# Split operands, one gate buffer and a later load of x in the stage that mixes the two branches of a diffusion layer

## The chip, the cores and the metric

The kernel runs on one core of one Trainium2 chip. The metric is the device time of one launch in microseconds (us). The profile is one execution of the same kernel, taken by the hardware profiler; its span is the time from the first to the last instruction.

## The reference, cut to what matters

One layer works on 1280 tokens (256 context tokens, 1024 latent ones) of 1024 features, all in float32. Two branches, an RWKV scan (`y_a`, 512 features) and an attention (`y_b`, 512 features), are projected, gated, summed and projected again. Then comes a feed-forward part of 2816 features.

```python
y_a, s_fin = rwkv_branch(r, k, v, xw, xa, xg, s0, lp)      # ends with a group norm, a bonus term and a gate
mixed = jax.nn.sigmoid(ga) * (y_a @ lp['w_out_a']) + jax.nn.sigmoid(gb) * (merge_heads(y_b) @ lp['w_out_b'])
x = x + g1 * (mixed @ lp['w_out'])
h2 = rmsnorm(x, lp['norm2_g']) * (1 + sc2) + sh2
x = x + g2 * conv_ffn(h2, lp)
```

The change is inside the line `mixed = ...`: two products with weights of 512 x 1024 each, for 1280 tokens.

## The kernel before, in words

Features lie on the 128 partitions and tokens along the free axis. So `y_a` (`ya`) and `y_b` (`yb4`) are 4 tiles of 128 x 1280 each, and `mixed` (`mix`) has 8 such tiles. A product for one output tile goes over the tokens in three segments (`SEGS`: 256, 512 and 512 columns), each with a PSUM bank of its own.

Two ways of multiplying are used. Most weight tiles (the input projection, `w_out`, the feed-forward part) go through `split_mm` (lines 876 to 880). Both operands are kept as a high part in the type float32r and a low part, the rest, in the same type. Three matmuls are issued for each product: high x high, high x low, low x high. The high parts of a weight are made by a multiplication with ones on GpSimd (line 2366) and the rest by a subtraction there (line 2367). Both are in `split_tile(s, loads, used, src)`. It waits for the load of the tile into one of the two buffers `raw[0]`, `raw[1]`, then for `w_used` (the PE has finished with the pair `hi[s]`, `lo[s]`), and counts up `w_split`. The mix alone multiplies plain float32: `mix_block(n)` (line 1347) takes its weights straight from `raw[q]` and its data from `ya` and `yb4`, 4 tiles deep for 3 segments, first the a half (q = 0), then the b half (q = 1). So 2 x 8 halves of 12 products each make the whole stage. The profile shows each float32 matmul as two records.

What stands around it, in the order of the PE's queue:

- Group norm of the scan's output (lines 1300 to 1341). For each of the 4 tiles j of `ya` the PE spreads the inverse deviations (`gn`, line 1338) and computes the gate (`gate`, line 1326). VectorE scales (line 2207, reads one SBUF tile and PSUM), adds bias and bonus (line 2210, reads two SBUF tiles) and multiplies by the gate (line 2213, SBUF and PSUM). `ya_ready` counts the last of these, `gn_out` the first. ScalarE has its last work of this stage at line 1771. GpSimd has none.
- The mix (lines 1347 to 1361). VectorE multiplies each half by its sigmoid gate from PSUM (line 2227, 3 instructions a half), adds the two (line 2233, two SBUF tiles) and counts `mix_ready`. ScalarE rounds the tile to its high part `mixH` (line 1779) and VectorE subtracts (line 2219, `mix_rest`, two SBUF tiles), one block later.
- The projection `w_out` (lines 1375 to 1398): 8 blocks of `split_mm`. In block n = 0 the loop over the 8 tiles k of `mix` is outermost, each waiting for its `mix_split`. From n = 1 on, the PE also transposes the input `x` (`x_again`) to features first, between the segments (line 1371).

SyncE issues all loads of this stretch in one fixed order. `load_mix(n, q)` brings one half's weights (256 KB) into the first half of `raw[q]`. `load_gates(n)` brings two tiles of 640 KB (line 817), into one of two buffers of two tiles each; it waits for `mix_ready` of the block two back. Five of the ten row blocks of `x` (512 KB each) are loaded behind block 1 of the mix (line 827), where their memory is free, and the other five behind the second load of `w_out` (line 840). That second load waits for the last matmul of the mix.

The memory of this stretch is packed. `gates` takes 4 tiles of 1280 words from `FREE + KB*T`, `x_again` lies over the same 8 tiles' space, `mixH` takes the 8 tiles ahead of it and `mix` the 8 behind it.

## Time and profile before

| what | value |
|---|---|
| time, median of 3 runs | 2513.81 us (2509.5, 2513.81, 2513.95) |
| profiled execution | 2510.51 us, span 2508.7 us |
| PE busy | 2377.6 us, 95% of the span |
| VectorE, ScalarE, GpSimd busy | 1302.6, 727.7 and 657.9 us |
| granted TensorE clock, mean | 0.983 of 2.4 GHz |
| traffic with memory | 234.5 MB, 93 GB/s over the span |

Engines are PE (TensorE matmul), PEld (its weight loads), DVE (VectorE), ACT (ScalarE), POOL (GpSimd) and SP (SyncE, which issues the loads; SPq is its queue). "L1354" is line 1354. In a timeline a row has start and duration in us, engine, line, operation, output<-inputs with shapes, the number of instructions merged into the row and, in brackets, how long the engine was idle before it and what released it. Matmuls are pipelined. One instruction's duration is longer than the distance to the next one's start, and the distance is what the engine spends.

### The profile page before, as it was taken

To read this page: it belongs to the slowest core of one execution; us is meant where nothing else is said; L and a number is where in the kernel's file an instruction comes from. 1 tells how busy PE (TensorE), PEld (TensorE's weight loads), DVE (VectorE), ACT (ScalarE), POOL (GpSimd) and SP (SyncE) were. 2 spreads that over 40 slices of the span, in tenths; PEclk is the share of its full clock that TensorE was granted. 3 is DMA by queue.
4 is the path that set the end of the run, shared out by engine and by line. 5 is a ranking of instruction groups with operands and counts; after the bars stand their busy time and mean duration, and the time that the engine had idled before them with its cause. 6 is when DMAs were issued, how large, how long until landed. Compare 5 with 4: busy or idle time off the path is not lost.

```text
span 2508.7 us, 50664 instructions
## 1 busy us (share of the span) xinstructions
PE 2377.6 (95%) x21610; PEld 1953.1 (78%) x21610; DVE 1302.6 (52%) x2069; ACT 727.7 (29%) x1193; POOL 657.9 (26%) x283
## 2 busy tenths in 40 slices
PE   5899999999999998889999998999999999999997
PEld 4677878788888887888855587788888888888885
DVE  4565657537468667895543424733333433343344
ACT  5273644544455553333300001301100110011002
POOL 1121020111111111222100144344344434444341
PEclk9899999999999999999989999999999999999999
DMA  6213121021366776676503311011111111111112
GB/s 281 89 46 115 45 70 62 28 94 66 103 193 188 207 203 206 178 215 178 178 31 133 130 43 34 26 43 34 43 34 42 40 37 43 34 43 34 43 34 93
DMA packets 224561, 234.53 MB, mean 93 GB/s; under 512 B 143922, under 2 KB 178866, under 8 KB 222898
## 3 DMA queue, kind: packets, MB, share of 16 engines
q1 hardware_dynamic: 199090, 229.55, 28.4%
q10 hardware_dynamic: 25344, 3.15, 0.8%
q8 instruction: 97, 1.59, 0.3%
q14 instruction: 30, 0.25, 0.0%
HBM read 173.80 MB, written 57.02 MB: 92 GB/s over the span
## 4 chain that ended last, share of the span: by engine, by line
PE 81%; DVE 9%; issue 3%; ACT 2%; DMA 2%; SPq 1%; ACTq 1%; POOL 1%; DVEq 0%; POOLq 0%
PE PS L878 19%; PE PS L880 19%; PE PS L879 19%; PE PS L1354 5%; PE PS L1022 3%; PE PS L994 2%; DVE buffer L2080 2%; DVE buffer L2081 2%; PE PS L1008 1%; PE PS L996 1%; PE PS L1326 1%; PE PS L1164 1%; PE PS L1074 1%; DMA buffer<-in_w_ada_first 1%; ACTq L1723 1%
## 5 line engine op out<-in xcount | busy, mean ns | idle before, releaser
L878 PE MATMUL PS<-buffer,buffer 128*128 128x512 f32 (+1 forms) x2784 | 994.6, 357 | 17.0 <-DVE buffer L2265 6.0
L880 PE MATMUL PS<-buffer,buffer 128*128 128x512 f32 (+1 forms) x2784 | 990.1, 356 | 0.0
L879 PE MATMUL PS<-buffer,buffer 128*128 128x512 f32 (+1 forms) x2784 | 987.3, 355 | 0.0
L878 PEld LDWEIGHTS PS<-buffer,buffer 128*128 128x128 f32 x2784 | 526.4, 189 | 106.1 <-issue 23.2
L879 PEld LDWEIGHTS PS<-buffer,buffer 128*128 128x128 f32 x2784 | 526.7, 189 | 78.0 <-issue 1.0
L880 PEld LDWEIGHTS PS<-buffer,buffer 128*128 128x128 f32 x2784 | 526.5, 189 | 73.2
L2366 POOL TENSOR_TENSOR buffer<-buffer,buffer 128x1024 fp32r<-128x1024 f32 x76 | 183.9, 2420 | 816.2 <-PE PS L880 506.3
L2309 DVE SCALAR_TENSOR_TENSOR buffer<-PS,buffer,buffer 128x512 f32<-128x512 f32 (+1 forms) x264 | 158.5, 656 | 148.3 <-PE PS L880 148.3
L2367 POOL TENSOR_TENSOR buffer<-buffer,buffer 128x1024 fp32r<-128x1024 f32 x76 | 194.2, 2556 | 6.0
L2285 DVE TENSOR_SCALAR buffer<-buffer,buffer 128x1281 f32<-128x1281 f32 x22 | 34.8, 1581 | 282.3 <-ACT buffer L1810 282.3
L1810 ACT ACTIVATE buffer<-PS 128x512 f32<-128x512 f32 (+1 forms) x66 | 30.1, 529 | 498.1 <-PE PS L880 498.1
L2379 POOL TENSOR_TENSOR buffer<-buffer,buffer 128x1024 fp32r<-128x1024 f32 x28 | 71.8, 2564 | 352.7 <-ACT buffer L1620 352.7
L1354 PE MATMUL PS<-buffer,buffer 128*128 128x512 f32 (+1 forms) x384 | 137.8, 521 | 0.8 <-DVE buffer L2213 0.8
L1354 PEld LDWEIGHTS PS<-buffer,buffer 128*128 128x128 f32 x384 | 72.9, 190 | 66.4 <-issue 60.7
L1022 PE MATMUL PS<-buffer,buffer 128*128 128x128 f32 x832 | 107.7, 277 | 4.3 <-DVE buffer L1976 4.3
L2348 POOL TENSOR_TENSOR buffer<-buffer,buffer 128x1024 fp32r<-128x1024 f32 x12 | 29.6, 2469 | 305.2 <-DMA buffer<-in_w_in 255.4
L1022 PEld LDWEIGHTS PS<-buffer,buffer 128*128 128x128 f32 x832 | 99.6, 192 | 6.9 <-DVE buffer L1976 6.9
L2388 POOL TENSOR_TENSOR buffer<-buffer,buffer 128x512 f32<-128x512 f32 x40 | 53.0, 1347 | 192.9 <-PE PS L1220 177.5
L1859 DVE CUSTOM_DVE_ANT_0 PS<-buffer,buffer 128x1024 f32<-128x1024 f32 x64 | 78.9, 1233 | 25.6 <-DMA buffer<-in_w_ada 21.1
L2294 DVE TENSOR_TENSOR buffer<-buffer,PS 128x512 f32<-128x512 f32 (+1 forms) x66 | 35.6, 594 | 106.8 <-PE PS L880 105.5
L2286 DVE SCALAR_TENSOR_TENSOR buffer<-buffer,buffer,buffer 128x1281 f32<-128x1281 f32 x22 | 77.0, 3502 | 2.6 <-DVE buffer L2285 1.4
L1573 ACT ACTIVATE buffer<-buffer,buffer 128x768 f32<-128x768 f32 (+1 forms) x80 | 67.9, 849 | 32.5 <-DVE buffer L1963 32.4
(226 smaller groups left out, 2793.6 us busy)
## 6 DMA issues: line engine op xcount, KB each, us to landing
buffer<-in_w_up SPq DMA_DIRECT2D x44, 512.0 KB, 3.4
buffer<-in_w_in SPq DMA_DIRECT2D x42, 512.0 KB, 5.3
ops_kept<-buffer SPq DMA_DIRECT2D x40, 512.0 KB, 4.6
buffer<-ops_kept SPq DMA_DIRECT2D x80, 256.0 KB, 3.5
buffer<-in_w_ada SPq DMA_DIRECT2D x32, 512.0 KB, 6.7
buffer<-rkv_kept SPq DMA_DIRECT2D x120, 128.0 KB, 3.4
buffer<-in_w_down SPq DMA_DIRECT2D x22, 512.0 KB, 3.3
buffer<-in_x SPq DMA_DIRECT2D x20, 512.0 KB, 6.9
```

Of the source, the lines that this page charges most:

```text
L878: mm(out, w_hi, x_hi, start=start, stop=False)
L879: mm(out, w_hi, x_lo, start=False, stop=False)
L880: return mm(out, w_lo, x_hi, start=False, stop=stop)
L1022: ins = mm(PS[:, 6, 0:P], src[:, at, :], pT[u % 2][:, b, :], start=(b == 0), stop=(b == nb - 1))
L1354: ins = mm(PS[:, 3 * q + g, 0:m], raw[q][:, k, :], src[:, k, t0:t0 + m], start=(k == 0), stop=(k == NP - 1))
L1573: act.activation(scr[:, u % 3, lo:768], scr[:, u % 3, lo:768], ACT.Exp, bias=rowstat[:, u % 3, 0:1], accum_out=rowstat[:, u % 3, 1:2]).the ...
L1859: return dve.tensor_tensor_reduce(spare, src, silu[:, c, :], 1.0, 0.0, ALU.mult, ALU.add, dst[:, c:c + 1])
L2286: V.link(stt(u, upad[:, odd, 0:ZP - 2], conv_taps("conv_ffn", f, 0), u, ALU.mult, ALU.add))
L2309: ins = stt(x1[:, n, t0:t0 + m], PS[:, 3 * (n % 2) + g, 0:m], mod[:, 40 + n, c:c + 1], x1[:, n, t0:t0 + m], ALU.mult, ALU.add)
L2366: G.link(pool.tensor_tensor(hi[s], src, ones_tile, ALU.mult))
L2367: pool.tensor_tensor(lo[s], src, hi[s], ALU.subtract).then_inc(w_split, 1)
L2379: pool.tensor_tensor(lo[t % 2], raw[t % 2], hi[t % 2], ALU.subtract).then_inc(w_split, 1)
```

## The change

The mix is computed as the other tiles are. Its weights of both halves are loaded into one `raw` buffer and split into `hi`, `lo` on GpSimd. `ya` and `yb4` are split too: the high part by ScalarE (`Copy` into float32r), the rest by GpSimd. `mix_block` uses `split_mm` and computes the b half first. There is one gate buffer of two tiles instead of two buffers. All ten row blocks of `x` are loaded behind the mix. The tile numbers behind the mix grow by 8 (`MIX_TILE`, `WO_TILE`).

```diff
+        ybH = view(FREE + KB * T, NP, T, dtype=F32R)
+        yaH = [view(FREE + (KB + NP) * T, 2, T, dtype=F32R), view(FREE + (KB - 2) * T, 2, T, dtype=F32R)]
+        ybL = view(KK_AT, NP, T, dtype=F32R)
+        yaL = view(LO_AT + NP * T, NP, T, dtype=F32R)
+        gates = view(FREE + (KB + NP + 2) * T, 2, T)
...
 SyncE
+            def load_mix(n):
+                r = (n + 1) % 2
+                if n >= 2:
+                    sp.wait_ge(w_split, MIX_TILE + n - 1)
+                for q in range(2):
+                    sp.dma_start(raw[r][:, q * NP:(q + 1) * NP, :].rearrange("p k n -> p (k n)"),
+                                 dram[("w_oa", "w_ob")[q]][n]).then_inc(w_in[r], 16)
...
             def load_gates(n):
-                if n >= 2:
-                    sp.wait_ge(mix_ready, n - 1)
+                if n == 0:
+                    sp.wait_ge(var_done, 1)
+                else:
+                    sp.wait_ge(mix_ready, n)
                 for q in range(2):
-                    sp.dma_start(gates[:, 2 * (n % 2) + q, :], dram["gates_kept"][q * KB + n]).then_inc(gates_in[n % 2], 16)
+                    sp.dma_start(gates[:, q, :], dram["gates_kept"][q * KB + n]).then_inc(gates_in, 16)
...
+            load_mix(1)
             load_gates(0)
-            load_gates(1)
             for n in range(1, KB):
+                if n + 1 < KB:
+                    load_mix(n + 1)
+                load_gates(n)
+            for n in range(KB):
+                load_tile(n % 2, dram["w_o"][n], WO_TILE + max(n - 1, 0))
                 if n == 1:
+                    for b in range(TB):
+                        if b == 0:
+                            sp.wait_ge(w_used, WO_TILE)
+                        if b == 7:
+                            sp.wait_ge(mix_ready, KB)
                         sp.dma_start(x_again[:, b, :], dram["x"][b]).then_inc(tiles_moved[b // 2], 16)
...
 TensorE
             def mix_block(n):
+                s = n % 2
+                pe.wait_ge(w_split, MIX_TILE + n + 1)
+                for at, (q, part) in enumerate(((1, yb_part), (0, ya_part))):
+                    if n == 0:
+                        pe.wait_ge((gn_out, ya_ready)[at], 3 * NP)
+                        pe.wait_ge(y_split, NP * (at + 1))
+                    else:
+                        pe.wait_ge(mix_out, 2 * n - 1 + at)
                     for g, (t0, m) in enumerate(SEGS):
                         for k in range(NP):
-                            ins = mm(PS[:, 3 * q + g, 0:m], raw[q][:, k, :], src[:, k, t0:t0 + m], start=(k == 0), stop=(k == NP - 1))
+                            x_hi, x_lo = part(k)
+                            ins = split_mm(PS[:, 3 * at + g, 0:m], hi[s][:, q * NP + k, :], lo[s][:, q * NP + k, :],
+                                           x_hi[:, t0:t0 + m], x_lo[:, t0:t0 + m], k == 0, k == NP - 1)
+                    ins.then_inc((mix_mm, w_used)[at], 1)
-            pe.wait_ge(ya_ready, 3 * NP)
-            pe.wait_ge(gn_out, 3 * NP)
-            pe.wait_ge(yb_kept, 32)
...
 ScalarE
+            act.wait_ge(yb_kept, 32)
+            for k in range(NP):
+                act.activation(ybH[:, k, :], yb4[:, k, :], ACT.Copy).then_inc(y_rounded, 1)
+            for k in range(NP):
+                act.wait_ge(ya_ready, 3 * k + 3)
+                act.activation(yaH[k // 2][:, k % 2, :], ya[:, k, :], ACT.Copy).then_inc(y_rounded, 1)
             for k in range(KB):
                 act.wait_ge(mix_ready, k + 1)
+                if k == KB - 2:
+                    act.wait_ge(w_used, WO_TILE)
                 act.activation(mixH[:, k, :], mix[:, k, :], ACT.Copy).then_inc(mix_rounded, 1)
...
 VectorE, mix_products(n): waits for gates_in, 32 * (n + 1); takes the b half first, gates[:, q], PS[:, 3 * at + g]
...
 GpSimd
+            def split_mix(n):
+                split_tile(n % 2, W4 + 2 * (n // 2) + 2, MIX_TILE + n - 1, raw[(n + 1) % 2])
+            def split_y(at, rest, whole, rounded):
+                pool.wait_ge(y_rounded, at)
+                pool.tensor_tensor(rest, whole, rounded, ALU.subtract).then_inc(y_split, 1)
+            split_mix(0)
+            for k in range(NP):
+                split_y(k + 1, ybL[:, k, :], yb4[:, k, :], ybH[:, k, :])
+            for k in range(NP):
+                split_y(NP + k + 1, yaL[:, k, :], ya[:, k, :], yaH[k // 2][:, k % 2, :])
             pool.wait_ge(gate_done, 3 * NP)
+            for n in range(1, KB):
+                split_mix(n)
```

## Rows read from the trace of the kernel before

**Rows 1.** Busy time by stretch: stretch, its length, busy us (count) by engine, granted clock, DMA share, GB/s.
```profile
1261.60:1293.70 32.10, 31.37 (x59) 13.27 (x58) 21.25 (x29) 1.77 (x4) 0.00 (x0) 0.63 0.00 0
1293.70:1431.50 137.80, 137.75 (x386) 73.19 (x387) 43.10 (x58) 8.89 (x7) 4.70 (x2) 1.00 0.31 107
1431.50:1552.70 121.20, 119.63 (x658) 102.72 (x657) 35.35 (x53) 10.62 (x9) 61.12 (x25) 1.00 0.19 66
```

**Rows 2.** The chain that ended last, in order of time (start, us, what), at the mix.
```profile
1293.75 137.76 PE PS L1354 x384
```

**Rows 3.** Groups of instructions by line: busy us, mean ns, idle before.
```profile
L1354 PE MATMUL PS<-buffer,buffer 128*128 128x512 f32 (+1 forms) x384 | 137.8, 521 | 0.8 <-DVE buffer L2213 0.8
```

**Rows 4.** Timeline of the mix.
```profile
1302.64 0.33 SPq L781 DMA_DIRECT2D buffer<-in_w_oa  x1
...
1311.23 0.33 SPq L781 DMA_DIRECT2D buffer<-in_w_ob  x1
...
1328.42 1.62 DVE L2227 TENSOR_TENSOR buffer<-buffer,PS 128x256 f32<-128x256 f32 x3 [6.91 <-PE PS L1354]
1330.08 1.49 DVE L2233 TENSOR_TENSOR buffer<-buffer,buffer 128x1280 f32<-128x1280 f32 x1
...
1331.60 0.80 SPq L817 DMA_DIRECT2D buffer<-gates_kept  x2
```

**Rows 5.** Timeline from the end of the mix.
```profile
1431.18 0.19 PEld L878 LDWEIGHTS PS<-buffer,buffer 128*128 128x128 f32 x1 [0.51 <-POOL buffer L2367]
...
1433.09 0.28 PE L878 MATMUL PS<-buffer,buffer 128*128 128x256 f32 x1
...
1434.61 5.09 DVE L2219 TENSOR_TENSOR buffer<-buffer,buffer 128x1280 fp32r<-128x1280 f32 x2
...
1434.81 0.28 PE L878 MATMUL PS<-buffer,buffer 128*128 128x256 f32 x1
...
1435.90 2.45 POOL L2366 TENSOR_TENSOR buffer<-buffer,buffer 128x1024 fp32r<-128x1024 f32 x1 [4.76 <-DMA buffer<-in_w_o]
...
1438.43 3.54 POOL L2367 TENSOR_TENSOR buffer<-buffer,buffer 128x1024 fp32r<-128x1024 f32 x1
...
1445.18 0.38 PE L1371 MATMUL PS<-buffer,buffer 128*128 128x128 f32 x2
```

**Rows 6.** Timeline of the group norm's end.
```profile
1265.89 1.50 ACT L1771 ACTIVATE buffer<-PS 8x256 f32<-8x256 f32 x3 [3.84 <-PE PS L1153]
...
1269.93 1.55 DVE L2210 SCALAR_TENSOR_TENSOR buffer<-buffer,buffer,buffer 128x1280 f32<-128x1280 f32 x1
...
1273.30 4.64 PE L1326 MATMUL PS<-buffer,buffer 128*128 128x256 f32 x6
...
1277.87 4.63 PE L1338 MATMUL PS<-buffer,buffer 8*128 8x256 f32 x6
...
1286.52 2.41 PE L1338 MATMUL PS<-buffer,buffer 8*128 8x256 f32 x6
...
1288.86 4.11 PE L1326 MATMUL PS<-buffer,buffer 128*128 128x256 f32 x6
...
1293.01 0.69 DVE L2213 TENSOR_TENSOR buffer<-buffer,PS 128x512 f32<-128x512 f32 x1 [0.65 <-PE PS L1326]
...
1293.75 41.52 PE L1354 MATMUL PS<-buffer,buffer 128*128 128x256 f32 x116 [0.78 <-DVE buffer L2213]
```

**Rows 7.** One line's instructions each: duration in ns min/median/max, first and last start.
```profile
L2219 DVE TENSOR_TENSOR buffer<-buffer,buffer x8: 1483/1485/3671, 1331.5 to 1436.0; 128x1280 fp32r<-128x1280 f32 x8
L2442 POOL TENSOR_TENSOR buffer<-buffer,buffer x22: 2890/2962/2981, 1613.2 to 2455.0; 128x1280 fp32r<-128x1280 f32 x22
```

**Rows 8.** Busy time by stretch, columns as in the first group, while gates are loaded.
```profile
1331.60:1337.00 5.40, 5.40 (x14) 2.46 (x13) 1.37 (x1) 1.27 (x1) 0.00 (x0) 1.00 0.66 243
```

**Rows 9.** The loads of the gates: time from issue to landing.
```profile
DMA to landing us min/median/max: 3.2/5.5/13.9
```

**Rows 10.** Busy time by stretch, while `x` is loaded behind the mix.
```profile
1437.00:1441.00 4.00, 4.00 (x22) 3.42 (x21) 2.70 (x1) 0.00 (x0) 3.92 (x2) 1.00 1.03 417
```

More of the change, by code:

```diff
@@ L489, in build @@
         assert FREE + 3 * KB * T == LO_AT
-        gates = view(FREE + KB * T, 4, T)
+        ybH = view(FREE + KB * T, NP, T, dtype=F32R)
[3 more added lines that the diff above has]
+        gates = view(FREE + (KB + NP + 2) * T, 2, T)
         mixH = view(FREE, KB, T, dtype=F32R)
@@ L518, in build @@
         tstat = view(FREE + 6 * D, 2, TB)
-        WO_TILE = len(TILES)
+        MIX_TILE = len(TILES)
+        WO_TILE = MIX_TILE + KB
         FFN_TILE = WO_TILE + KB
@@ L546, in build @@
             sem(n) for n in ("mix_mm", "mix_out", "mix_ready", "mix_rounded", "mix_split"))
-        gates_in = [sem(f"gates_in{s}") for s in range(2)]
+        gates_in = sem("gates_in")
+        y_rounded, y_split = sem("y_rounded"), sem("y_split")
         xt_done, xt_out, x1_out = (sem(n) for n in ("xt_done", "xt_out", "x1_out"))
@@ L795, in _ @@
                     sp.wait_ge(w_split, len(TILES))
-                    load_mix(0, 1)
+                    load_mix(0)
                 if i == 5:
@@ L809, in _ @@
             sp.wait_ge(fin_stored, 16)
-            load_mix(0, 0)
             def load_gates(n):
-                if n >= 2:
-                    sp.wait_ge(mix_ready, n - 1)
+                if n == 0:
+                    sp.wait_ge(var_done, 1)
+                else:
+                    sp.wait_ge(mix_ready, n)
                 for q in range(2):
-                    sp.dma_start(gates[:, 2 * (n % 2) + q, :], dram["gates_kept"][q * KB + n]).then_inc(gates_in[n % 2], 16)
+                    sp.dma_start(gates[:, q, :], dram["gates_kept"][q * KB + n]).then_inc(gates_in, 16)
             sp.dma_start(yb4.rearrange("p j t -> p (j t)"), dram["yb_kept"]).then_inc(yb_kept, 16)
+            load_mix(1)
             load_gates(0)
-            load_gates(1)
             for n in range(1, KB):
-                for q in range(2):
-                    load_mix(n, q)
-                if n == 1:
-                    for b in range(TB // 2, TB):
-                        sp.dma_start(x_again[:, b, :], dram["x"][b]).then_inc(tiles_moved[b // 2], 16)
-                if n + 1 < KB:
-                    load_gates(n + 1)
-            for n in range(KB):
-                if n < 2:
-                    sp.wait_ge(mix_mm, 2 * KB - 1 + n)
-                    load_tile(n, dram["w_o"][n])
-                else:
-                    load_tile(n % 2, dram["w_o"][n], WO_TILE + n - 1)
-                if n == 1:
-                    for b in range(TB // 2):
-                        sp.wait_ge(mix_ready, KB - 1 if b < 2 else KB)
+                if n + 1 < KB:
[3 more added lines that the diff above has]
+                load_tile(n % 2, dram["w_o"][n], WO_TILE + max(n - 1, 0))
+                if n == 1:
+                    for b in range(TB):
[3 more added lines that the diff above has]
+                            sp.wait_ge(mix_ready, KB)
                         sp.dma_start(x_again[:, b, :], dram["x"][b]).then_inc(tiles_moved[b // 2], 16)
@@ L2222, in mix_products @@
                 out = mix[:, n, :]
-                dve.wait_ge(gates_in[n % 2], 32 * (n // 2 + 1))
-                for q, dst in enumerate((out, gates[:, 2 * (n % 2) + 1, :])):
-                    dve.wait_ge(mix_mm, n * 2 + q + 1)
+                dve.wait_ge(gates_in, 32 * (n + 1))
+                for at, (q, dst) in enumerate(((1, gates[:, 1, :]), (0, out))):
+                    if at == 0:
+                        dve.wait_ge(mix_mm, n + 1)
+                    else:
+                        dve.wait_ge(w_used, MIX_TILE + n + 1)
                     for g, (t0, m) in enumerate(SEGS):
-                        ins = tt(dst[:, t0:t0 + m], gates[:, 2 * (n % 2) + q, t0:t0 + m], PS[:, 3 * q + g, 0:m], ALU.mult)
+                        ins = tt(dst[:, t0:t0 + m], gates[:, q, t0:t0 + m], PS[:, 3 * at + g, 0:m], ALU.mult)
                         if g < 2:
@@ L2232, in mix_products @@
                 dve.wait_ge(mix_out, n * 2 + 2)
-                tt(out, out, gates[:, 2 * (n % 2) + 1, :], ALU.add).then_inc(mix_ready, 1)
+                tt(out, out, gates[:, 1, :], ALU.add).then_inc(mix_ready, 1)
             dve.wait_ge(ya_ready, 3 * NP)
```

14 lines of the change are left out of this document (4 added, 10 removed).

## The prediction, made before the changed kernel ran

> **What bounds the kernel now.** I read the busy time by stretch first. From 1293.70 to 1431.50 us the PE is busy 137.75 of 137.80 us at a granted clock of 1.00 (its upper level, 2.4 GHz), VectorE 43.10 us, ScalarE 8.89 us, GpSimd 4.70 us, and DMA runs at 0.31 of its engines [rows 1]. The chain that ended last says the same: one piece of 137.76 us, all of it matmuls of the mix [rows 2], and the group of that line has 0.8 us of idle time in the whole launch [rows 3]. So the mix is bound by the PE alone, and only what its matmuls cost, and what then fails to keep up with them, matters. The group norm before it is no such place: the PE has a mean clock of 0.63 there and VectorE is busy 21.25 of 32.10 us [rows 1], in a chain that goes back and forth between the two. Behind the mix the PE is busy 119.63 of 121.20 us [rows 1], so time saved in the mix reaches the end.
>
> **The matmuls.** A half of the mix takes from one release of its weights to the next: 1302.64 to 1311.23, 8.59 us [rows 4], for 4 tiles x 3 segments in float32. The split form is seen right behind the mix: the first 256-column matmul of one tile k starts at 1433.09, that of the next at 1434.81 [rows 5], 1.72 us for 3 segments x 3 matmuls. With its start, the block of 8 such tiles takes 1431.18 to 1445.18, 14.0 us, or 1.75 a tile [rows 5]. I take 1.725. A half is 4 tiles deep, 4 x 1.725 = 6.90 us. Shapes, types and clock are the same there as in the changed mix. The gain is 16 x (8.59 - 6.90) = **27.0 us**; with 1.75 it would be 25.4.
>
> **Splitting the weights.** GpSimd splits 8 tiles more, 2.45 us and about 2.4 us each. In steady state tile n+1 is split from the end of block n-1 on and wanted one block, 13.8 us, later. Hidden, with some 7 us to spare, also where VectorE holds it up. Tile 0 is split at the end of the scan, tile 1 behind the splits of `ya`. The first `w_out` tile's split now falls inside the last mix block, since the load no longer waits for a mix half. That removes the wait of 0.51 us of the weight load for line 2367, some 0.3 us of it PE time [rows 5]: **-0.3 us**.
>
> **Splitting ya and yb.** ScalarE does 8 `Copy`s of 1280 columns at the 1.27 us its present rounding takes [1.27 busy in rows 8], GpSimd 8 subtractions at 2.96 us [rows 7]. The b half's four start behind ScalarE's last norm work, which ends at 1265.89 + 1.50 = 1267.4 [rows 6], and would be done at 1268.7 + 4 x 2.96 = 1280.5 if nothing held them, long before the PE wants them. Of the a half the last counts: `ya` is complete at 1293.01 + 0.69 = 1293.7 [rows 6], + 1.3 + 2.96 makes 1298.0. The b half gives cover: it need not wait for `ya`, only for the PE's own gate matmuls, which end at 1288.86 + 4.11 = 1292.97 [rows 6]. So the PE starts 0.78 us earlier [rows 6] and reaches the a half at 1292.97 + 6.90 = 1299.9, 1.9 us behind its data. Doing the b half first turns 4.3 us of waiting into nothing.
>
> **What the splits cost VectorE.** This is the term that I had to bound. No GpSimd work lies in the norm stage now (0.00 us, rows 1). Line 2219 shows what happens when both read two SBUF tiles. Seven of its eight take about 1.485 us, one takes 3.671 [rows 7]. That one started just behind a GpSimd instruction (1435.90, 2.45 us), and GpSimd's next one was stretched to 3.54 us by it [rows 5]. Each held the other off. Line 2210, four times 1.55 us in the norm's chain [rows 6], also has two SBUF inputs, and each now meets a busy GpSimd. Lower end: none is held, 0. Upper end: all four are, by 3.671 - 1.485 = 2.19 us each, and all of it in the chain, 8.8 us. I replayed the stage with that mutual holding. The first hold delays the second gate matmuls (1273.30, rows 6) by about 1.8 us. The second one is swallowed, since VectorE then waits for the PE's slow 4.63 us norm matmuls anyway (1277.87, rows 6). The third and fourth add some. The PE then starts the mix at 1295.1 instead of 1293.75, **+1.4 us** net of the 0.78 gained. `ya` is complete at 1297.6 and split at about 1302.0, just as the b half ends. For that tie I add **+0.5 us**.
>
> The Trainium skill, page "SBUF — State Buffer", section "Who interferes with whom", says that a VectorE instruction with two SBUF inputs and a GpSimd instruction that reads SBUF exclude each other for the whole instruction, whichever starts first. It speaks against this change: a hold could last a full 2.96 us, four of them 11.8 us, and the gain would be near 15.5 us. The trace agrees on the exclusion (3.671 against 1.485 us) but has only that one case at this place, with a hold of 2.19 us.
>
> **One gate buffer.** With E for the PE's end of a block, VectorE multiplies the a half and adds: `mix_ready` comes 1.62 + 1.49 us behind E now [rows 4]. In the changed kernel GpSimd's split starts at E too, and the addition waits for its first instruction, so E + 4.0. Then the gates are issued. The present pair, issued at 1331.60 [rows 4], is moved by 1337.00: 5.40 us x 243 GB/s = 1.31 MB, the two tiles [rows 8]. So they land at E + 9.4, VectorE multiplies the b half (wanted at E + 6.9, so late) until E + 11.1, and the PE needs those banks at E + 13.8. It is hidden by **2.7 us**, cost 0. If a load took longer than 5.4 + 2.7 = 8.1 us, the excess would be paid in each of 7 blocks. The median to landing is 5.5, the longest 13.9 us [rows 9]. I put the 13.9 down to the first pairs, which are issued right behind the load of `yb` (4 tiles of 0.655 MB); in the changed kernel only the first pair could meet that, and it is wanted only at 1302. In SyncE's queue the next weights stand behind a gate load, not ahead of it, so they don't delay it.
>
> **x behind the mix.** Ten loads of 0.524 MB at 417 GB/s [rows 10] are 12.6 us, with start and the wait of b = 7 for `mix_ready` (E + 3 to 4) all land by about E + 15. The transposes start at E + 14.0 (1445.18 against 1431.18, rows 5) with the first two row blocks, the last four are wanted some 8.5 us later. The next `w_out` tile queues behind: landed at about E + 17, split by E + 22, wanted at E + 28.9. Cost 0. High rounding of the last two tiles of `mix` must wait for E: they are wanted at E + 10.3 and E + 12.1, and VectorE has its rests done by E + 10. Cost 0.
>
> **Sum.** -27.0 - 0.3 + 1.4 + 0.5 = **-25.4 us**. Against the profiled execution, 2510.51 us (span 2508.7), that is 2485.1. The four times shown of before (with the profiled one 2509.5, 2510.51, 2513.81 and 2513.95) fall in two groups, so I take their mean of 2511.9 as base: **2486.5 us**.
>
> **Rivals.**
> 1. *The norm stage pays more.* All four holds in the chain (+8.8, less the 0.8), or the clock. The third norm spread ran 4.63 us at half clock and the last one 2.41 us at the upper level [rows 6]. If the added waits cost that spell, +2.2 us, and +2 to 3 more if the mix begins at half clock. For it: the four two-input instructions are in the chain. Against: one of them sits where VectorE waits anyway. The sum is then -27.3 + 8.0 to 13, so -14 to -19: 2493 to 2498. The Trainium skill, "TensorE: Matmul & The Clock Gate", Part 1, says that the clock is throttled by default and that activity releases it; more waiting would go that way, and the trace agrees in that this stage has the mean of 0.63.
> 2. *Gate loads are late by a little.* At 10 us to landing, 1.9 us x 7 = 13 us are given back: 2500. For it: the spread of landings. Against: the 5.4 us of the pair in this very place.
> 3. *Slower than before.* The same place: from a landing of 8.1 + 25.4 / 7 = 11.7 us on, the single buffer costs more than the matmuls give. At the longest one seen, 13.9 us, it costs 5.8 x 7 = 41 us: 2527. For it: such a landing is in the trace. Against: the median of the 16 is 5.5 us.
> 4. *It doesn't do what it says.* A float32r matmul with fresh weights each time could cost more here than behind the mix. The tiles and segments are the same, so the time would be 2511 only if something else paced the PE.
>
> **How the numbers follow.** The forecast within 3 us 0.75; rival 1 0.13; rival 2 0.05; rival 3 0.03; rival 4 0.02; a little better than forecast (no holds) 0.02. What a measurement of this kernel can tell from no change is about 0.2%, 5 us. The range goes from no hold at all and a base of 2509.5 (2482) to the dearer part of rival 1 (2496). Faster 0.95, same 0.02, slower 0.03.
>
> **What would show it.** L880's group grows by 192, half a mix period is 6.90 us, the PE is busy without a gap from the first mix matmul to the norm behind `w_out`, line 2210 takes over 3 us at least twice, the mix starts 1 to 3 us later than 1293.75. A PE gap for lines 2227 (banks) in each block would mean rival 2 or 3, a gap ahead of the first a half that the tie went wrong, one for the transposes that x is late.

## The result, and the profile after

The changed kernel takes 2494.32 us (median of 4 runs, 2490.52 to 2500.85) against 2513.31 us (4 runs of before, 2509.5 to 2513.95, on the same chip). The ratio is 0.9941 with a 95% interval of 0.992 to 0.9962, so some 15 us are gained by the ratio (19 by the two medians) where 25.4 were forecast, and the median lies 7.8 us above the predicted 2486.5. The execution profiled is the slowest of the four, 2500.85 us (span 2499.1).

First the busy time by stretch of the changed kernel, as in [rows 1]: the end of the norm from its first gate matmul on, the mix, and `w_out`'s stage.

```profile
1263.70:1293.03 29.33, 25.16 (x59) 11.90 (x60) 23.48 (x26) 10.21 (x11) 22.05 (x7) 0.73 0.17 63
1293.03:1407.21 114.18, 111.10 (x579) 94.14 (x577) 65.08 (x66) 10.20 (x8) 49.95 (x19) 0.99 0.32 115
1407.21:1528.70 121.49, 119.92 (x657) 102.95 (x657) 35.71 (x50) 10.62 (x9) 62.18 (x25) 1.00 0.22 81
```

The mix takes 114.18 us instead of 137.80, a PE that was busy without a gap now has 3.08 us of gaps, and GpSimd is in the norm with 22.05 us. The groups of the matmul lines within 1263.7 to 1410 us say which gaps these are:

```profile
L882 PE MATMUL PS<-buffer,buffer 128*128 128x512 f32 (+1 forms) x197 | 70.2, 356 | 3.1 <-POOL buffer L2391 1.9 <-POOL buffer L2431 1.2
```

1.9 us for the first `w_out` tile's low part (L2391) and 1.2 us for a low part of `ya` (L2431). With them the mix, taken with `w_out`'s first block, still gave 23.3 of the 26.8 us forecast for it. To find the rest, both spans are cut at the same five events:

| us | to the first gate matmul | norm to the first mix matmul | mix and `w_out`'s first block | `w_out`'s other blocks | from the first `ms` matmul to the end | span |
|---|---|---|---|---|---|---|
| before | 1261.5 | 32.2 | 151.5 | 107.5 | 956.0 | 2508.7 |
| after | 1263.7 | 29.3 | 128.2 | 107.5 | 970.4 | 2499.1 |

"Gate", "mix" and "`ms`" stand for the PE's first matmul at each (`ms` is the one for the mean square behind `w_out`); the FFN is the feed-forward part. **14.4 us are lost behind all changed work**, in the FFN, which the diff doesn't touch. The first column, also ahead of the change, differs by chance: it lies between 1256 and 1264 us in the fourteen profiles of this study, whatever the kernel. The list of PE's waits from 1600 to 2400 us in the changed kernel has one line (us in total, times, longest):

```profile
PE PS L883 <- issue: 6.9, 4, 2.0
```

Before has none there. The chain that ended last gives the four places (start, us, what):

```profile
1772.42 1.98 issue
...
1942.41 1.77 issue
...
2108.94 1.43 issue
...
2275.29 1.72 issue
```

They lie 166 to 170 us apart, once in each pass of the FFN loop. The PE's timeline at the first of them, and its stretches of 4 us there (length, busy us, granted clock, DMA share, GB/s):

```profile
1770.91 0.39 PE L884 MATMUL PS<-buffer,buffer 128*128 128x512 f32 x1
1771.33 0.38 PE L882 MATMUL PS<-buffer,buffer 128*128 128x256 f32 x1
...
1772.14 0.28 PE L882 MATMUL PS<-buffer,buffer 128*128 128x256 f32 x1
1774.40 0.28 PE L883 MATMUL PS<-buffer,buffer 128*128 128x256 f32 x1 [1.98 <-issue]
```

```profile
1770.00:1774.00 4.00, 2.39 (x13) 1.00 0.01 4
1774.00:1778.00 4.00, 3.60 (x20) 0.69 0.15 31
1778.00:1782.00 4.00, 4.00 (x17) 0.88 0.29 104
```

The old pass ends with 512-column matmuls; with 256 columns the new one begins. It does seven matmuls and then stands for 1.98 us, waiting for no semaphore. Within 1771.9 to 1774.3 us the only DMA of the core is this:

```profile
q8 instruction: 1, 0.02, 2.4%
```

One packet of instructions is moved, and from what follows it is a block of the PE's program. A finer cut puts it within 20 ns of 1772.05 us. That is before the PE runs out of matmuls and 2.3 us before it goes on (2.1 to 2.7 us at the other jumps and at the first of `before_pad121` below). So if this is the block that is missing, the transfer itself isn't what takes the time; what the PE waits for behind it no view shows. And the stop costs more than itself: behind it the granted clock is 0.69 and then 0.88. How much more shows where ScalarE begins a turn's `h` (the same line, twice a turn):

```profile
1757.52 1.36 ACT L1831 ACTIVATE buffer<-PS 128x256 f32<-128x256 f32 x3 [38.45 <-PE PS L884]
1789.24 1.36 ACT L1831 ACTIVATE buffer<-PS 128x256 f32<-128x256 f32 x3 [14.91 <-PE PS L884]
```

31.72 us, where an undisturbed such interval is 27.5 to 27.7. The four intervals with a stop are 31.72, 29.58, 29.29 and 31.18 us, together 11.4 us over four of 27.6. The other 3 us of the 14.4 are no loss at the FFN's entry: from the first `ms` matmul to the first `h` it takes 43.5 us in both. They lie in the pace of the turns: six of the ten long intervals of a turn take 55.17 to 55.42 us where the first profile of before has 54.74, and their short ones are longer too, some 4 us in all, of which 1.2 come back behind the last `h`. That pace is taken up under `pad135` and `before_look`.

### The profile page after: what moved, and what is told of

It reads as the page before. It is cut to its first block, busy times and chain, and to the rows that moved or that the text cites. A ratio compares the mean times of both kernels' runs of the same rounds, so it can differ in the third digit from the quotient of the medians.

```text
span 2499.1 us, 51082 instructions
## 1 busy us (share of the span) xinstructions
PE 2353.3 (94%) x21802; PEld 1979.5 (79%) x21802; DVE 1326.4 (53%) x2069; ACT 737.1 (29%) x1201; POOL 729.9 (29%) x307
## 3 DMA queue, kind: packets, MB, share of 16 engines
q8 instruction: 98, 1.61, 0.3%
## 4 chain that ended last, share of the span: by engine, by line
PE 79%; DVE 10%; issue 4%; ACT 2%; DMA 2%; SPq 1%; POOL 1%; ACTq 1%; DVEq 0%; POOLq 0%
PE PS L882 21%; PE PS L883 21%; PE PS L884 21%; PE PS L1026 3%; PE PS L998 2%; DVE buffer L2102 2%; PE PS L1012 2%; DVE buffer L2101 1%; PE PS L1000 1%; ACTq L1736 1%; PE PS L1168 1%; PE PS L1078 1%; DMA buffer<-in_w_ada_first 1%; DVE buffer L1984 1%; PE PS L1069 0%
## 5 line engine op out<-in xcount | busy, mean ns | idle before, releaser
L882 PE MATMUL PS<-buffer,buffer 128*128 128x512 f32 (+1 forms) x2976 | 1067.5, 359 | 22.1 <-DVE buffer L2289 6.0
L883 PE MATMUL PS<-buffer,buffer 128*128 128x512 f32 (+1 forms) x2976 | 1057.2, 355 | 6.9 <-issue 6.9
L884 PE MATMUL PS<-buffer,buffer 128*128 128x512 f32 (+1 forms) x2976 | 1056.8, 355 | 0.0
L882 PEld LDWEIGHTS PS<-buffer,buffer 128*128 128x128 f32 x2976 | 562.5, 189 | 118.4 <-issue 28.0
L884 PEld LDWEIGHTS PS<-buffer,buffer 128*128 128x128 f32 x2976 | 562.7, 189 | 88.9 <-issue 7.3
L883 PEld LDWEIGHTS PS<-buffer,buffer 128*128 128x128 f32 x2976 | 563.1, 189 | 80.7 <-issue 1.5
L2390 POOL TENSOR_TENSOR buffer<-buffer,buffer 128x1024 fp32r<-128x1024 f32 x84 | 203.9, 2427 | 683.8 <-PE PS L884 560.4
L2391 POOL TENSOR_TENSOR buffer<-buffer,buffer 128x1024 fp32r<-128x1024 f32 x84 | 220.0, 2619 | 6.6
L2403 POOL TENSOR_TENSOR buffer<-buffer,buffer 128x1024 fp32r<-128x1024 f32 x28 | 71.6, 2556 | 353.3 <-ACT buffer L1633 353.3
L2372 POOL TENSOR_TENSOR buffer<-buffer,buffer 128x1024 fp32r<-128x1024 f32 x12 | 29.6, 2465 | 308.0 <-DMA buffer<-in_w_in 259.0
L1026 PEld LDWEIGHTS PS<-buffer,buffer 128*128 128x128 f32 x832 | 99.9, 193 | 6.5 <-DVE buffer L1997 6.5
L1880 DVE CUSTOM_DVE_ANT_0 PS<-buffer,buffer 128x1024 f32<-128x1024 f32 x64 | 78.9, 1233 | 26.8 <-DMA buffer<-in_w_ada 22.3
L1984 DVE TENSOR_REDUCE buffer<-buffer 128x1 f32<-128x768 f32 (+1 forms) x80 | 67.7, 846 | 17.1 <-ACT buffer L1566 13.6
L1837 ACT ACTIVATE buffer<-buffer 128x1280 f32<-128x1280 f32 x22 | 28.1, 1275 | 163.8 <-DVE buffer L2313 163.8
```

Of the source, the lines that this page charges most:

```text
L882: mm(out, w_hi, x_hi, start=start, stop=False)
L883: mm(out, w_hi, x_lo, start=False, stop=False)
L884: return mm(out, w_lo, x_hi, start=False, stop=stop)
L1026: ins = mm(PS[:, 6, 0:P], src[:, at, :], pT[u % 2][:, b, :], start=(b == 0), stop=(b == nb - 1))
L1880: return dve.tensor_tensor_reduce(spare, src, silu[:, c, :], 1.0, 0.0, ALU.mult, ALU.add, dst[:, c:c + 1])
L1984: dve.tensor_reduce(rowstat[:, u % 3, 0:1], scr[:, u % 3, lo:768], AX.X, ALU.max, negate=True) \
```

## The experiments

**Theory A**, the loop's place. The PE's program is fetched in blocks of 16.4 KB (the instruction queue's 98 packets hold 1.61 MB), and a block is taken to hold 256 instructions; `before_pad121` tests that number too. The change makes the program in front of the loop longer: PE and PEld each go from 21610 to 21802 instructions, 384 more. Its waits are 7 fewer, so 377 = 256 + 121. The loop itself is unchanged, 1768 instructions. It moves by 121 within the blocks, and after it the jump back lands 18 instructions (seven matmuls with their weight loads) ahead of a block's end. By the theory, the next block isn't there yet. **Rival B**: the new instructions leave something else behind (a queue, the clock, buffer addresses) that slows the FFN. Waits on a constant that has long been reached move the loop. Two in the code are one instruction in the program: `range(64)` makes 51114 instructions of 51082. Up to 153 of them cost nothing at the FFN's entry, where the first `h` still comes 43.5 us behind the first `ms` matmul; 216 do, see `pad216`. **Theory C**, beside them: the 1.9 us at the mix's end come from the order of SyncE's queue. **Theory D**: the stretched norm chain is GpSimd's and VectorE's mutual holding. The texts recorded ahead of the runs call A theory F, C theory Q and D theory L; theory R there is the chance of one execution.

**`same`**: the changed kernel, nothing edited.

> The changed kernel once more, unchanged, five rounds. Theory F (instruction fetch): in the feed-forward loop the PE jumps back to a place that has only about 7 matmuls left before the next 16 KB of its instructions; it runs these and then waits 1.4 to 2.0 us for the fetch, and the clock falls to half for some us behind it, 1.8 to 4.0 us for each of the four jumps back. It belongs to the program, so the four waits come again at the same matmul and the time is 2489 to 2501. Theory R (chance of one execution): the profile that was read was a poor one; here the waits are gone or elsewhere, and the time is near 2488.

2497.24 us (2492.95 to 2502.47, 6 runs), ratio 0.9948 (0.9932 to 0.9964). Its profile has the stops again, 1.74, 1.46, 1.94 and 1.40 us. The last stretch is 967.2 us, the mix with `w_out`'s first block 126.9, the norm 30.5. The four jump turns together are 7.8 us longer than four of 27.49.

**`w_o_early`**: the first two `w_out` tiles are issued ahead of the last block's gates.

```diff
                 if n + 1 < KB:
                     load_mix(n + 1)
+                else:
+                    for m in range(2):
+                        load_tile(m, dram["w_o"][m], WO_TILE)
                 load_gates(n)
...
-                load_tile(n % 2, dram["w_o"][n], WO_TILE + max(n - 1, 0))
+                if n >= 2:
+                    load_tile(n % 2, dram["w_o"][n], WO_TILE + n - 1)
```

> The changed kernel with the first two loads of w_out issued ahead of the last gates' load instead of behind it. Theory Q (order in SyncE's queue): the PE's wait of 1.9 us ahead of the w_out stage, released by the split on GpSimd, came from the load standing behind a gates' load that waits for mix block 6; it goes to 0 and the kernel is 1.9 us (0.08%) faster than the unchanged one of this call. Rival: the split is late for another reason (GpSimd held off by VectorE), then the wait stays over 1 us.

2495.11 us (6 runs), ratio 0.9944 (0.9927 to 0.9961). The times alone don't tell it from `same`; the trace does. In the changed kernel, around the mix's end:

```profile
1391.64 1.62 DVE L2251 TENSOR_TENSOR buffer<-buffer,PS 128x256 f32<-128x256 f32 x3 [2.64 <-PE PS L884]
...
1394.81 0.80 SPq L826 DMA_DIRECT2D buffer<-gates_kept  x2
1395.65 1.30 SPq L633 DMA_DIRECT2D buffer<-in_w_o  x2
1400.97 1.62 DVE L2251 TENSOR_TENSOR buffer<-buffer,PS 128x256 f32<-128x256 f32 x3 [4.78 <-DMA buffer<-gates_kept]
1402.32 2.39 POOL L2390 TENSOR_TENSOR buffer<-buffer,buffer 128x1024 fp32r<-128x1024 f32 x1 [18.25 <-DMA buffer<-in_w_o]
...
1407.21 0.38 PE L882 MATMUL PS<-buffer,buffer 128*128 128x256 f32 x1 [1.89 <-POOL buffer L2391]
```

The `w_out` load stands in SyncE's queue behind the last gate load, which waits for the block before to be added up (`mix_ready`). So it is issued only at 1395.65 us, GpSimd begins at 1402.32, and the PE waits 1.89 us. In `w_o_early`:

```profile
1390.53 0.80 SPq L826 DMA_DIRECT2D buffer<-gates_kept  x2
...
1400.45 2.43 POOL L2394 TENSOR_TENSOR buffer<-buffer,buffer 128x1024 fp32r<-128x1024 f32 x1 [7.69 <-PE PS L888]
```

Now GpSimd waits for the PE to be through with the tile before, no longer for a load, the 1.89 us are gone, and the piece takes 124.7 us. The forecast for it was 151.5 - 27.0 - 0.3 + 0.5 = 124.7, and to meet it so well is chance: the same edit in `early_pad32` below has 127.1. C holds for the wait of 1.89 us. The last stretch stays at 966.0 us with its four stops (2.00, 1.54, 1.97, 2.00): they are no matter of this queue.

**`no_split_reads`**: GpSimd reads nothing for the low parts of `ya` and `yb` (these are left out of the computation).

```diff
-                pool.tensor_tensor(rest, whole, rounded, ALU.subtract).then_inc(y_split, 1)
+                pool.memset(rest.bitcast(F32), 0.0).then_inc(y_split, 1)
```

> The changed kernel where GpSimd's eight subtractions for the low parts of ya and yb are memsets to zero: the low parts are left out of the result, all waits and their order stay, but GpSimd reads nothing from SBUF there. Theory L (mutual holding): the four two-input VectorE instructions of the norm stage take 1.55 us each again instead of 3.0, 3.6, 3.6 and 3.9, the mix starts up to 4 us earlier and the a half of block 0 is not waited for (1.2 us): 3 to 5 us faster than the unchanged one. Rival: VectorE's instructions are back to 1.55 us but the stage is no shorter, since the PE's slow matmuls pace it: under 2 us.

2491.98 us (6 runs), ratio 0.9927 (0.9911 to 0.9943). The line of VectorE that has two SBUF inputs in the norm's chain (ns min/median/max; first and last start), in the changed kernel and then here:

```profile
L2231 DVE SCALAR_TENSOR_TENSOR buffer<-buffer,buffer,buffer x4: 2994/3564/3882, 1272.0 to 1292.3; 128x1280 f32<-128x1280 f32 x4
```

```profile
L2231 DVE SCALAR_TENSOR_TENSOR buffer<-buffer,buffer,buffer x4: 1551/1552/1552, 1264.5 to 1280.2; 128x1280 f32<-128x1280 f32 x4
```

All four are held while GpSimd reads, none without. D holds. The norm takes 25.9 us here, instead of 30.5 in `same` and 29.3 in the first profile of the changed kernel; the granted clock of that stage differs too, 0.77 here, 0.67 and 0.73 there, so not all of the difference need be the holding. That a VectorE instruction with two SBUF inputs and a reading GpSimd exclude each other is also what the Trainium skill says, page "SBUF — State Buffer", section "Who interferes with whom"; the trace agrees, with 2.99 to 3.88 us against 1.55.

**`pad32`**: 32 instructions more ahead of the loop.

```diff
+            for _ in range(64):
+                pe.wait_ge(consts_in, 32)
             ffn_up(0, 0)
```

> The changed kernel with 32 waiting instructions more in the PE's program, on a semaphore long satisfied, placed where the PE idles ahead of the feed-forward part, so that the loop starts 32 instructions later in the program. Theory F: the jump back now lands just behind a 16 KB boundary with some 240 instructions to go, the four waits vanish and the kernel is 7 to 11 us faster than the unchanged one: about 2480 to 2484. Theory R: no difference from the unchanged one within 2 us.

2483.61 us (2479.74 to 2488.41, 5 runs), ratio 0.9891 (0.9873 to 0.9908), where `same` has 0.9948 against the same runs of before: 13.6 us by the medians for 32 instructions that do nothing. The last stretch is 956.1 us, as before the change, with no stop. ScalarE's turn at the jump is 27.49 us:

```profile
1755.32 1.37 ACT L1833 ACTIVATE buffer<-PS 128x256 f32<-128x256 f32 x3 [38.12 <-PE PS L884]
1782.81 1.37 ACT L1833 ACTIVATE buffer<-PS 128x256 f32<-128x256 f32 x3 [10.79 <-PE PS L884]
```

The instruction queue from 1600 to 2400 us moved this, in the changed kernel and in `pad32`:

```profile
q8 instruction: 42, 0.69, 0.4%
```

```profile
q8 instruction: 6, 0.10, 0.1%
```

This place does more than spare a stop: the loop is hardly fetched again at all. The 36 packets fewer, over 800 us or 4.8 passes, are 7 to 8 a pass, as many as a loop of 1768 instructions has blocks of 256.

**`before_pad121`**: the reverse, 121 instructions into the kernel before, none of the change.

```diff
+            for _ in range(242):
+                pe.wait_ge(consts_in, 32)
             ffn_up(0, 0)
```

> The kernel before with 121 waiting instructions more in the PE's program, on a semaphore long satisfied, where the PE idles ahead of the feed-forward part. Its loop then starts at the place inside a 16 KB block of instructions at which the changed kernel's loop starts (the change moved it by 377 instructions, 377 - 256 = 121); nothing of the change itself is in it. Theory F: the four waits of 1.4 to 2.0 us behind the jumps back appear in the kernel before, 7 matmuls into the turn, and it becomes 8 to 14 us slower: ratio 1.003 to 1.006. Rival (the waits belong to the changed data, buffers or loads): no difference, within 2 us, beside at most 1 us for the added instructions.

2521.1 us (2514.82 to 2527.49, 8 runs), ratio 1.0037 (1.0022 to 1.0053): 9.3 us slower by the ratio. The stops are there at each jump, the first of them again behind the seventh matmul:

```profile
1789.44 0.28 PE L878 MATMUL PS<-buffer,buffer 128*128 128x256 f32 x1
...
1790.15 0.28 PE L878 MATMUL PS<-buffer,buffer 128*128 128x256 f32 x1
1792.25 0.28 PE L879 MATMUL PS<-buffer,buffer 128*128 128x256 f32 x1 [1.82 <-issue]
```

B falls: the stop comes with the place, whether the mix is split or not. A holds for the place; that the stop is a wait for the fetch is argued from the packets and from how far the block's end is. A move by 377 and one by 121 end behind the same seventh matmul, so their difference, 256 instructions, is a whole number of blocks, and with the packets of `pad32` it is one.

**`early_pad32`** has both edits, `w_o_early` and `pad32`.

> The changed kernel with the 32 waiting instructions and with the first two loads of w_out ahead of the last gates' load. If the two repairs are independent, 2483.6 - 1.8 = about 2482, with no wait over 0.5 us ahead of w_out and none behind the jumps back. Rival: the wait for the load hides another of the same size, then 2483.6.

2484.21 us (2478.78 to 2489.8, 4 runs), ratio 0.9896 (0.9881 to 0.9912); the profiled execution has a span of 2477.0 and a last stretch of 954.8 us. By its time it is no better than `pad32`, whose 0.9891 it was to undercut by some 2 us; that is within the intervals. In the profiles the norm, the mix and `w_out`'s first block together take 156.4 us, where `pad32` has 159.1, so the saving is there in the stage that was edited; 1.8 us of it is the wait for the first `w_out` tile.

**`early_pad32_yb_ahead`**: in addition ScalarE rounds `yb` before it waits for the norm's variance, so that GpSimd starts its reads earlier.

```diff
+            act.wait_ge(yb_kept, 32)
+            for k in range(NP):
+                act.activation(ybH[:, k, :], yb4[:, k, :], ACT.Copy).then_inc(y_rounded, 1)
             act.wait_ge(var_done, 1)
...
-            act.wait_ge(yb_kept, 32)
-            for k in range(NP):
-                act.activation(ybH[:, k, :], yb4[:, k, :], ACT.Copy).then_inc(y_rounded, 1)
```

> As early_pad32, and ScalarE rounds the four tiles of yb ahead of its wait for the variances, so that GpSimd's first four subtractions run before the norm's last part instead of beside it. Theory L (mutual holding costs the norm stage 5 us, as the version without the reads showed): two or three of the four two-input VectorE instructions are held less, and it is 1.5 to 4 us faster than early_pad32, about 2479. Rival: the splits of ya alone hold all four as before, or the earlier subtractions hold line 2212 instead: within 1 us of early_pad32.

2478.57 us (2476.84 to 2483.81, 4 runs), ratio 0.9872 (0.9856 to 0.9887). The line that was held, here:

```profile
L2237 DVE SCALAR_TENSOR_TENSOR buffer<-buffer,buffer,buffer x4: 1551/3870/3878, 1267.0 to 1286.5; 128x1280 f32<-128x1280 f32 x4
```

One of the four is free, the others are held a little longer; the norm takes 28.5 us instead of 29.3. The norm, the mix and `w_out`'s first block together take 154.3 us (154.4 in `best_again`) where `early_pad32` has 156.4, so some 2 us are gained there. Against `early_pad32` the intervals overlap, and the profiled spans are only 0.5 us apart, so the rest of the step from 0.9896 to 0.9872 isn't explained.

**`pad216`**: as `pad32` with `range(432)`, 216 instructions. The jump lands 58 instructions, some 27 matmuls, ahead of a block's end.

> The changed kernel with 216 waiting instructions instead of 32: the loop starts some 58 instructions (27 matmuls, 3.2 us) ahead of a 16 KB boundary instead of some 18 (7 matmuls, 0.8 us). Theory F, in which a fetch takes about 0.8 + 2.0 = 2.8 us from the jump on: the waits behind the jumps vanish or are under 0.4 us. If the fetch takes longer than that, a wait stands 27 matmuls into the turn. The added instructions may cost up to 3 us where they don't fit the idle time.

2490.91 us (2 runs, 2486.6 and 2495.22), ratio 0.9916 (0.9895 to 0.9937). With 27 matmuls to do meanwhile nothing of the stops is left that the list of waits would show; the turn intervals at the four jumps are 27.83, 27.74, 27.62 and 27.49 us, though 42 blocks are fetched in 800 us as in the changed kernel. So it isn't the fetching that costs, it is having only seven matmuls' time for it. The last stretch is still 963.6 us, 7.5 more than in `pad32`, and most of it is the price of the added waits themselves: at the FFN's entry (1250 to 2510 us, PE's waits: us in total, times, longest) stands

```profile
PE PS L882 <- issue: 20.8, 1, 20.8
```

instead of one wait of 6.2 us in `pad32`, and the first `h` comes 49.5 us behind the first `ms` matmul instead of 43.5. So 216 waits cost 6.0 us there, where up to 3 were expected. The remaining 1.5 us are turns at the slower pace.

**`pad135`**: `range(270)`. With 377 + 135 = 512 the loop stands in its blocks as in the kernel before.

> The changed kernel with 135 waiting instructions, which with the 377 that the change moved the loop by makes 512, two whole 16 KB blocks: the loop starts at the same place inside a block as in the kernel before, and still spans 8 blocks. The profiles so far show 42 fetches of 16 KB in 800 us of the loop for the kernel before, the changed one and pad216, and 6 for pad32, whose loop spans 7 blocks. Theory F (the wait depends on how many instructions are left in the first block): the fetches go on, 41 or 42, but none is waited for, the part behind w_out takes 956 us as before, and the kernel is 26 us faster than before (ratio 0.989 to 0.991), as pad32 was. Rival G (pad32 gained because its loop is never fetched again): pad135 keeps waits behind the jumps and stays at 2490 or more.

2490.18 us (2487.3 to 2493.47, 5 runs), ratio 0.992 (0.9906 to 0.9934). No stop, again 42 fetches, so rival G of the expectation, by which the waits stay, falls. But the time that theory A (F there) gave for it, 0.989 to 0.991, was missed: it is 6 to 7 us above `pad32`, and its last stretch is 964.3 us, not 956.1. The added waits cost nothing at the entry (43.5 us again). ScalarE's turns say where: the long interval of a turn, 54.74 us in `pad32`, is longer in most turns here. In `pad135`, ahead of a jump and behind it:

```profile
1696.82 1.36 ACT L1833 ACTIVATE buffer<-PS 128x256 f32<-128x256 f32 x3 [10.91 <-PE PS L884]
1752.23 1.37 ACT L1833 ACTIVATE buffer<-PS 128x256 f32<-128x256 f32 x3 [38.67 <-PE PS L884]
1780.26 1.37 ACT L1833 ACTIVATE buffer<-PS 128x256 f32<-128x256 f32 x3 [11.20 <-PE PS L884]
1835.00 1.37 ACT L1833 ACTIVATE buffer<-PS 128x256 f32<-128x256 f32 x3 [38.19 <-PE PS L884]
```

55.41 us ahead of the jump, 54.74 us behind it, at a granted clock of 1.00 in both. A third value, 55.17, is seen elsewhere. Over ten such intervals and the ten short ones between them (27.49 or 27.73 us) the paces differ by up to 9 us. The theory formed here, **H**: the pace belongs to a loop that is fetched again and again, so a loop that stays (as in `pad32`) is faster by it, in the kernel before too.

**`best_again`**: `early_pad32_yb_ahead` once more.

> early_pad32_yb_ahead once more, beside pad135 on one chip: 2478 to 2481, which is 3 to 6 us under pad135 if the earlier load of w_out (1.9 us) and the earlier splits of yb (1 to 2 us) are real; within 1 us of it if they are not.

2479.07 us (2475.97 to 2489.94, 6 runs), ratio 0.9882 (0.9863 to 0.99). The best version holds, 1.2% faster than before.

**`before_pad153`**: 153 instructions (`range(306)`) into the kernel before put its loop where `pad32` has it.

> The kernel before with 153 waiting instructions in the same place: its loop then starts where pad32's does, just behind a 16 KB boundary, and spans 7 blocks instead of 8. Nothing of the change is in it. pad135 had no wait over 0.6 us behind its jumps, yet most of its turns took 55.41 us where pad32 and the one profile of the kernel before show 54.74. Theory H: that slower pace belongs to a loop whose instructions are fetched again in every turn, and the kernel before has it too in most executions, its profile being a lucky one. Then this kernel is 4 to 9 us faster than before (ratio 0.9965 to 0.9985), with about 6 fetches in 800 us of the loop and all turns at 54.74. Rival: the kernel before has no slow turns; then the ratio is 1.000 within 0.001.

2509.56 us (2498.87 to 2515.92, 12 runs), ratio 0.9994 (0.9979 to 1.0009). The loop does stay (7 packets in 800 us), and all long intervals of its profile are 55.17 us. **H falls**: a loop that isn't fetched again is no faster than one whose fetches are covered, by more than the interval's 5 us.

**`before_look`**: the kernel before, unchanged, profiled a second time.

> The kernel before once more, for a second profile. Theory H: some of its ten long intervals of the loop take 55.17 or 55.41 us instead of 54.74, and the part behind w_out over 957 us. Rival: all at 54.74 and 956 again.

2509.66 us (1 run), span 2507.4, last stretch 960.5 us against 956.0 in the first profile, with turns such as this:

```profile
1637.74 1.36 ACT L1810 ACTIVATE buffer<-PS 128x256 f32<-128x256 f32 x3 [10.90 <-PE PS L880]
1692.91 1.36 ACT L1810 ACTIVATE buffer<-PS 128x256 f32<-128x256 f32 x3 [38.37 <-PE PS L880]
```

55.17 us, in a kernel whose first profile had no slow turn. So the pace differs between executions of one kernel. In the nine profiles of a loop that is fetched again it changes only at a jump back; in the five of a loop that stays it doesn't change at all (54.74 us throughout in four, 55.17 in `before_pad153`). What sets it stays open, and with it whether the 7 us of `pad135` against `pad32` are more than chance.

What each place of the loop does, in one table ("start" is the loop's first instruction within its 256-instruction block; counted from the programs, with the blocks' ends put where the stops fall):

| kernel | start | instructions to the block's end | blocks the loop touches | stops | packets, 1600 to 2400 us | last stretch, us |
|---|---|---|---|---|---|---|
| before | 117 | 139 | 8 | none | 42 | 956.0, 960.5 |
| after, `same` | 238 | 18 | 8 | 1.40 to 1.98 us | 42 | 970.4, 967.2 |
| `before_pad121` | 238 | 18 | 8 | 1.72 to 2.08 us | 41 | 972.0 |
| `pad216` | 198 | 58 | 8 | none listed | 42 | 963.6 |
| `pad135` | 117 | 139 | 8 | none | 42 | 964.3 |
| `pad32` | 14 | 242 | 7 | none | 6 | 956.1 |
| `before_pad153` | 14 | 242 | 7 | none | 7 | 960.7 |

The two last rows explain the packets: 1768 instructions fit into seven blocks only where the start is at 24 or less. The 963.6 us of `pad216` hold 6.0 us for its own waits.

The Trainium skill, page "Runtime: NRT & Kernel Launch", section "Instruction fetch mechanics", says that instructions are refilled in blocks of 16 KiB and that a taken branch to a block that isn't held stalls the engine. The traces agree with the size (16.4 KB a packet). They show a stall at each jump back (1.40 to 2.08 us), but not at the branch's target: seven matmuls run there first, and the stall stands at the end of that block.

## Why the prediction was right and where it failed

- **The sign and the mechanism: right.** Half a mix period was forecast at 6.90 us. VectorE's products of the a halves start at 1377.94, 1391.64 and 1405.35 us in the changed kernel, 13.70 us a block, so 6.85 a half. By that period the term of -27.0 us was 0.8 too small; by the PE's busy time in the mix, 137.75 against 111.10 us, it was 0.3 too large; the mix now begins at a granted clock of 0.88 in its first 5 us, where before had 1.00. The float32r matmuls with fresh weights cost here what they cost behind the mix (rival 4 falls).
- **One gate buffer, cost 0: right.** The last pair of gates is multiplied at 1391.6 + 9.4 = 1401.0 us, exactly the E + 9.4 of the sum. VectorE does wait there, 4.78 us for the DMA, and the PE never does. Rivals 2 and 3 needed landings later by more than 2.7 us and did not come.
- **x behind the mix, cost 0: right.** The rest of `w_out`'s stage takes 107.5 us in both, though the median landing over all 20 loads of `x` rose from 6.9 to 8.1 us.
- **The first `w_out` tile, -0.3: wrong**, +1.9 instead (+1.6 in `same`). The step says that its split "falls inside the last mix block, since the load no longer waits for a mix half". It was moved behind another wait, the gate load's, and the sum priced the buffer and not the queue. `w_o_early` shows it.
- **The holding, +1.4: wrong in its parts.** I let the second of four holds be swallowed and asked for "over 3 us at least twice"; three are over 3 us and the fourth is 2.99, and a hold reaches 3.88 us where the sum had 3.67 at most. Still the norm took 29.3 us, 2.9 less than in the first profile of before. That is no gain of the change: the kernel before has 32.2 us at a granted clock of 0.63 in that stage (also in `before_pad153`), or 27.6 at 0.76 (`before_look`; 27.5 in `before_pad121`). The changed one has 29.3 at 0.73 and 30.5 to 31.5 at 0.62 to 0.67, and without the reads 25.9 at 0.77. So the reads cost 3.4 to 4.6 us by these profiles, the clock's part included, and whether the stage as a whole became longer depends on which profile of before it is held against. The forecast took one execution's clock in that stage for the stage's own.
- **The tie at the first a half, +0.5: 1.2** in the profiled execution, 0.4 in `same`.
- **The step that failed in size**: "Behind the mix the PE is busy 119.63 of 121.20 us (rows 1), so time saved in the mix reaches the end." It reaches the FFN, and there the loop's new place cost 11.4 us in the profiled execution. The sum put at nothing what a longer program does to the unchanged loop behind it: of the 576 matmuls in place of the plain ones it counted the run time, and nothing of their being instructions. None of the rivals had this place. `before_pad121`, which adds only the place, is 9.3 us slower than before, and `pad32`, the changed kernel with another place, is 13.6 us faster than `same`.
- **What the change is worth with the place taken out.** `pad32`'s 27 us against before aren't that number, since its loop stands where the loop of before never did. Kernels with the same place are the fair pairs: at 238, 0.9941 and 0.9948 against 1.0037 give 24 and 22 us; at 14, 0.9891 against 0.9994 gives 26; at 117, `pad135` against before gives 20. The ratios' intervals leave some 4 to 6 us either way. The profiles say much the same: norm, mix and `w_out`'s first block take 157.4 to 159.1 us in the changed kernel where these stages are as in `same`, and 179.0 to 183.7 in the one before. So the forecast of 25.4 was at the upper end, and two of the terms that it had wrong, the 1.9 us of the first `w_out` tile and the norm's clock, are on that side.
- **The range** of 2482 to 2496 was hardly wide enough, and its upper end was made for another reason. The median of the first four runs lies 1.7 us inside it. The ratio 0.9941 on the base of 2511.9 is 2497.1, and the six runs of `same` have 2497.24, both outside.

## What to carry to other kernels

When a change makes the program ahead of a loop longer or shorter, the loop moves within the blocks in which it is fetched, and that is worth looking at before the change is judged: count the instructions that the engine issues between the loop's start and its block's end, and where they are few, move the loop with some that do nothing, and check what these cost themselves (32 to 153 cost nothing here, 216 cost 6.0 us). Look for waits with no releaser at the loop's period, in stages that the change doesn't touch. And when a load is taken from behind one wait, read what else stands ahead of it in its queue.

## What the runs showed of the hardware that was not expected

- Seven matmuls of 256 columns, then 1.40 to 2.08 us of standing at every jump back, and a granted clock of 0.69 and 0.88 in the two stretches of 4 us behind: 1.6 to 4.1 us a jump against a turn of 27.6. A packet of instructions is moved 2.1 to 2.7 us before the PE goes on. With some 27 matmuls ahead of the block's end, the turns at the jumps take 27.5 to 27.8 us.
- A PE loop of 1768 instructions is fetched again in each pass when it lies in eight blocks (41 or 42 packets in 800 us) and stays when it lies in seven (6 or 7 packets).
- The same turn of the same loop takes 54.74, 55.17 or 55.41 us at a granted clock of 1.00, differently from one execution to the next. It changes only at a jump back, and not at all where the loop isn't fetched again.
- The group norm's stage has two lengths, with its granted clock, in one and the same kernel, 32.2 us at 0.63 and 27.6 us at 0.76.
